# A mixture-of-experts block on one core: the last pair of experts and the last norm written out by themselves

## The reference

```python
h = rms_norm(x, norm1_g);  proj = h @ w_in            # q, k, v, u
sb = rms_norm(stick_breaking_attention(q, k, v));  pool = multiscale_pool(u)
x = x + concat([sb, pool]) @ w_out
h2 = rms_norm(x, norm2_g)
# top 4 of 32 experts per token, softmax over the 4 logits
gu = h2 @ w_gate_up[e] + b_gate_up[e]                 # 1024 -> 2048
gate = minimum(gu[:, :1024], 7);  up = clip(gu[:, 1024:], -7, 7)
y_e = ((up + 1) * gate * sigmoid(1.702 * gate)) @ w_down[e] + b_down[e]
x = x + sum over the token's experts of gate_weight * y_e
return rms_norm(x, final_norm_g)
```

## Time and profile before

| | |
|---|---|
| median of 3 runs | 1057.35 us |
| the profiled execution, its own time | 1059.32 us |
| its span, first to last instruction | 1057.5 us |
| TensorE busy | 993.2 us (94%) |
| VectorE, ScalarE, GpSimd busy | 214.3, 129.3, 8.6 us |
| DMA | 418.43 MB, mean 396 GB/s |
| granted TensorE clock, mean | 0.995 |

### The profile page before, as it was taken

How to read it: one execution, slowest core, us unless ns; L and a number is a source line. 1 busy time by engine, 2 the same in 40 slices (tenths; PEclk the granted TensorE clock), 3 DMA queues, 4 the chain that set the end, 5 groups by cost and what they waited for, 6 DMA issues and landing times.

```text
span 1057.5 us, 11316 instructions
## 1 busy us (share of the span) xinstructions
PE 993.2 (94%) x4595; PEld 421.6 (40%) x4595; DVE 214.3 (20%) x479; ACT 129.3 (12%) x200; POOL 8.6 (1%) x27
## 2 busy tenths in 40 slices
PE   8999999999999999999999989899999989898996
PEld 6684534343433333333333333333334333333333
DVE  2134421112111111111212111111112121111104
ACT  2452200101010001010101000010001010010002
POOL 0001000000000000000000000000000000000000
PEclk9999999999999999999999999999999999999999
DMA  9955379999999999999999999999999999999992
GB/s 326 409 231 195 143 317 420 414 404 428 428 427 426 429 429 429 428 428 430 428 429 428 428 429 428 428 428 429 429 429 428 426 431 429 428 428 428 430 429 115
DMA packets 37826, 418.43 MB, mean 396 GB/s; under 512 B 4600, under 2 KB 5136, under 8 KB 10160
## 3 DMA queue, kind: packets, MB, share of 16 engines
q1 hardware_dynamic: 36320, 417.35, 93.8%
q10 hardware_dynamic: 1488, 0.82, 0.3%
HBM read 417.10 MB, written 1.05 MB: 395 GB/s over the span
## 4 chain that ended last, share of the span: by engine, by line
PE 59%; DMA 32%; DVE 4%; issue 2%; ACT 2%; ACTq 0%; DVEq 0%; SPq 0%
PE bank L942 58%; DMA ring<-in_w_gate_up_dram 32%; DVE area L831 1%; DVE area L828 1%; PE bank L1281 1%; DVE area L781 1%; DMA area<-in_norm_g_dram 1%; DVE area L835 1%; ACT area L526 0%; DVE sel L598 0%; PE bank L965 0%; DVE xn L920 0%; ACT area L447 0%; ACT area L445 0%; ACT area L443 0%
## 5 line engine op out<-in xcount | busy, mean ns | idle before, releaser
L942 PE MATMUL bank<-ring,area 128*64 128x512 f32 (+1 forms) x3088 | 701.2, 597 | 36.8 <-DMA ring<-in_w_gate_up_dram 30.4
L942 PEld LDWEIGHTS bank<-ring,area 128*64 128x64 f32 (+1 forms) x3088 | 220.9, 138 | 484.8 <-issue 410.5
L825 DVE TENSOR_SCALAR area<-bank 128x512 f32<-128x512 f32 x32 | 22.1, 692 | 472.9 <-PE bank L942 472.9
L524 ACT ACTIVATE area<-area 128x512 f32<-128x512 f32 x32 | 20.2, 630 | 503.9 <-DVE area L825 503.9
L942 PE MATMUL bank<-masks,xn 128*128 128x128 f32 x544 | 73.0, 288 | 1.0 <-issue 0.2
L942 PEld LDWEIGHTS bank<-masks,xn 128*128 128x128 f32 x544 | 66.7, 196 | 17.9 <-issue 14.1
L840 DVE COPY wide<-bank 64x512 f32<-64x512 f32 x32 | 22.2, 694 | 205.6 <-PE bank L942 205.6
L529 ACT ACTIVATE wide<-bank 64x512 f32<-64x512 f32 x32 | 18.9, 590 | 254.7 <-PE bank L942 254.7
L942 PE MATMUL bank<-area,ring 128*128 128x256 f32 x192 | 42.0, 380 | 0.3 <-DVE area L616 0.3
L942 PEld LDWEIGHTS bank<-area,ring 128*128 128x128 f32 x192 | 36.3, 190 | 5.4 <-DVE area L616 0.6
L942 PE MATMUL bank<-bias,sel 64*128 64x512 f32 x128 | 37.2, 641 | 0.0
(11 more groups left out here) (137 smaller groups left out, 289.4 us busy)
## 6 DMA issues: line engine op xcount, KB each, us to landing
ring<-in_w_gate_up_dram SPq DMA_DIRECT2D x112, 2048.0 KB, 31.7
ring<-in_w_down_dram SPq DMA_DIRECT2D x56, 2048.0 KB, 35.3
ring<-in_w_gate_up_dram SPq DMA_DIRECT2D x28, 1024.0 KB, 12.5
ring<-in_w_down_dram SPq DMA_DIRECT2D x14, 1024.0 KB, 11.9
ring<-in_w_in_dram SPq DMA_DIRECT2D x8, 512.0 KB, 10.1
ring<-in_w_in_dram SPq DMA_DIRECT2D x4, 1024.0 KB, 18.5
ring<-in_w_out_dram SPq DMA_DIRECT2D x4, 1024.0 KB, 16.9
area<-in_w_gate_up_dram SPq DMA_DIRECT2D x4, 1024.0 KB, 8.1
```

The source lines that it names most:

```text
L524: a.activation(sig, gatec, ACT.Sigmoid, scale=ALPHA).then_inc(sig_ok, 1)
L825: v.tensor_scalar(gatec, gbank[:], LIMIT, None, ALU.min).then_inc(gc, 1)
L942: return t.matmul(o, l, r, start=start, stop=stop, skip_group_check=True)
```

## The change

- The loops end one step earlier. Experts 28 and 29 are written out as they were; experts 30 and 31 have a part of their own (`last_pair`), without a gather behind 31.
- SyncE loads expert 31 in twelve transfers of 1 MB (`load_last`); TensorE waits for each chunk by itself.
- The rows of 30 and 31 are no longer added together. Each expert has a scatter matrix whose 64 slots stand in both halves of the partitions (`pick_twice`, `info_one`, `scatter_one`), and `ylast` puts one half of its columns on partitions 0 to 63, the other on 64 to 127. `combine_one` does four matmuls of 64 rows by 512 columns, alternately on the two halves of the array's rows. Expert 30's come after 31's up steps, 31's at the end.
- The residual is added by four matmuls of the identity with `xres` (`add_tokens`) after the second up step of 31.
- The gain's row goes half after the fourth up step, half after `combine_one(0)`, and ScalarE copies the halves into `fgrow` (`last_gains`), ahead of the sigmoid of expert 31 in its order. The warm-up of the root's table now stands before the copy of expert 31's rows.
- Banks 0 to 3 become one tile `acc`. ScalarE squares 1024 elements at a time right out of it, with no addition of two sums; the last rows are made by VectorE (`fin`) and, for a quarter, by a product of VectorE (`fmul`) and a scaled copy of ScalarE (`fin_a`). Three stores: 512 KB and 256 KB from SyncE, 256 KB from ScalarE.
- In the path not taken, semaphores are renamed.

```diff
+            c = HALF * (r ^ half)
+            return wide[half * SLOTS:(half + 1) * SLOTS, c:c + HALF]
         hidT_all = wide[:].rearrange("p (a b) -> p a b", a=KF)
         wpool = sb("wpool", [P, NG, GC])
         wrouter = sb("wrouter", [P, KD, NE])
...
+
             for r in range(BODY):
                 first_expert(r)
-            with sp.Fori(1, NBODY) as i:
+            with sp.Fori(1, NBODY - 1) as i:
...
-                sp.dma_start(out[0, tt * P:(tt + 1) * P, c:c + HALF],
-                             xn[:, tt, c:c + HALF]).then_inc(out_done, 16)
-            sp.wait_ge(out_done, 64)
+            for r in range(BODY - 1):
+                load_expert(NE - BODY + r, r * PER_EXPERT)
+            load_last(NE - 1, (BODY - 1) * PER_EXPERT)
+            sp.wait_ge(fin, 1)
+            sp.dma_start(out[0, 0:P, :], xn[:, 0, :]).then_inc(out_done, 16)
+            sp.wait_ge(fin, 2)
```

ScalarE and VectorE:

```diff
+            def last_gains():
+
+                for c in (1, 0):
+                    act.wait_ge(gain_ok, 2 - c)
+                    a.activation(fgrow[:, c * HALF:(c + 1) * HALF], (BU, BM)[c][:], ACT.Copy).then_inc(
+                        gain_c, 1)
...
+                fast_hidden(NE - 2)
+                act.wait_ge(chunks_used, (NE - 1) * PER_EXPERT)
+                a.activation(ylast(0, 0), BY[0:SLOTS, :], ACT.Copy).then_inc(y30, 1)
+                last_gains()
+                fast_hidden(NE - 1)
+                a.activation(stat[:, 15:16], epsc[:], ACT.Sqrt).then_inc(warm, 1)
+                act.wait_ge(chunks_used, NE * PER_EXPERT)
+                a.activation(ylast(1, 0), BY[0:SLOTS, :], ACT.Copy).then_inc(y31, 1)
+
+            for tt in range(TT):
+                act.wait_ge(sum_ok, tt + 1)
+                if tt == 1:
+
+                    act.wait_ge(fmul, 1)
+                a.activation(xn[:, tt, :], acc[:, tt, :], ACT.Square,
+                             accum_out=stat[:, 8 + tt:9 + tt]).then_inc(fsq, 1)
+                act.wait_ge(fsq, tt + 1)
                 a.activation(stat[:, 10 + tt:11 + tt], stat[:, 8 + tt:9 + tt], ACT.Sqrt,
                              scale=1.0 / D, bias=epsc[:]).then_inc(frt, 1)
...
+            act.wait_ge(finv, 2)
+            a.activation(xn[:, 1, 0:HALF], xres[:, 1, 0:HALF], ACT.Copy,
+                         scale=stat[:, 11:12]).then_inc(fin_a, 1)
+            act.wait_ge(fin_a, 1)
+            act.dma_start(out[0, P:2 * P, 0:HALF], xn[:, 1, 0:HALF]).then_inc(out_done, 16)
...
+            def pick_twice(e, p):
+
+
+                for tt in range(TT):
+                    for r in range(2):
+                        d = v.tensor_scalar(pick[p][:, tt, r * SLOTS:(r + 1) * SLOTS],
+                                            iota[:, 1:SLOTS + 1], rank[:, tt, e:e + 1], None,
+                                            ALU.is_equal)
+                d.then_inc(pick_ok, 1)
+
+            def scatter_one(r, p):
+
+
+                n = NE // 2 + 1 + r
+                dve.wait_ge(info_ok, n)
+                v.tensor_copy(info[:], BM[:, 0:3]).then_inc(info_c, 1)
+                dve.wait_ge(info_c, n)
+                v.tensor_scalar(scat[p], iota[:], info[:, 2:3], info[:, r:r + 1], ALU.is_equal,
+                                ALU.mult).then_inc(scat_ok, 1)
+
...
+                fast_pair(NE // 2 - 2, 0)
+
+                pick_twice(NE - 2, 0)
+                pick_twice(NE - 1, 1)
+                clamped(NE - 1)
+                choose_bias(NE - 1)
+                scatter_one(0, 1)
+                dve.wait_ge(comb_ok, NE // 2 - 1)
+                dve.wait_ge(scat_ok, NE // 2 + 1)
+                scatter_one(1, 0)
+                dve.wait_ge(chunks_used, (NE - 1) * PER_EXPERT)
+                v.tensor_copy(ylast(0, 1), BY[SLOTS:P, :]).then_inc(y30, 1)
+                clamped(NE)
+                dve.wait_ge(chunks_used, NE * PER_EXPERT)
+                v.tensor_copy(ylast(1, 1), BY[SLOTS:P, :]).then_inc(y31, 1)
...
+            dve.wait_ge(gain_c, 2)
+            dve.wait_ge(sum_ok, 2)
+            v.tensor_tensor(xres[:, 1, 0:HALF], bank[2], fgrow[:, 0:HALF], ALU.mult).then_inc(fmul, 1)
             final_inverse(0)
-            rows_final(0, 0)
-            sum_squares(1)
-            rows_final(0, 1)
+
+            v.scalar_tensor_tensor(out=xn[:, 0, :], in0=acc[:, 0, :], scalar=stat[:, 10:11], in1=fgrow,
+                                   op0=ALU.mult, op1=ALU.mult).then_inc(fin, 1)
             final_inverse(1)
-            rows_final(1, 0)
-            rows_final(1, 1)
+            v.scalar_tensor_tensor(out=xn[:, 1, HALF:D], in0=bank[3], scalar=stat[:, 11:12],
+                                   in1=fgrow[:, HALF:D], op0=ALU.mult, op1=ALU.mult).then_inc(fin, 1)
```

TensorE:

```diff
+            def final_gain(c):
+
+                for r in (2 * c, 2 * c + 1):
+                    m = mm((BU, BM)[c][:, (r % 2) * S:(r % 2 + 1) * S],
                            ident[NE:NE + 4, NE + r:NE + r + 1].to_broadcast([4, P]), fg,
                            start=(r % 2 == 0), stop=(r % 2 == 1))
                 m.then_inc(gain_ok, 1)
...
+            def info_one(r, p):
+
+                n = NE // 2 + 1 + r
+                pe.wait_ge(pick_ok, n)
+                pe.wait_ge(info_c, n - 1)
+                for tt in range(TT):
+                    m = mm(BM[:, 0:3], pick[p][:, tt, :], gtab[:, tt, NE // 2 - 1, :],
+                           start=(tt == 0), stop=(tt == 1))
+                m.then_inc(info_ok, 1)
+
+            def combine_one(r, p, done):
+
+
+                pe.wait_ge(scat_ok, NE // 2 + 1 + r)
+                pe.wait_ge((y30, y31)[r], 2)
+                for tt in range(TT):
+                    for hf in range(2):
+                        m = mm(bank[2 * tt + hf], scat[p][hf * SLOTS:(hf + 1) * SLOTS,
+                                                          tt * P:(tt + 1) * P],
+                               ylast(r, hf), stop=(r == 1))
+                    if r == 1:
+                        m.then_inc(done, 1)
+                if r == 0:
+                    m.then_inc(done, 1)
+
+            def add_tokens():
+
+                for tt in range(TT):
+                    for hf in range(2):
+                        mm(bank[2 * tt + hf], ident[:], xres[:, tt, hf * HALF:(hf + 1) * HALF])
+
+            def last_pair():
+
+                i, q = NBODY - 1, NE // 2 - 1
+                e = NE - 2
+                add_bias_of(e)
+                pe.wait_ge(xb_ok, q + 1)
+                m0 = 2 * PER_EXPERT
+                for k in range(KD):
+                    up_step(i, m0 + k, False, k, 1, slice(0, SLOTS)).then_inc(chunks_used, 1)
+                combine(q - 1, 0)
+                turn_hidden(e)
+                info_one(0, 0)
+                down(i, e, m0, False)
+
+                e = NE - 1
+                add_bias_of(e)
+                m0 = 3 * PER_EXPERT
+                info_one(1, 1)
+                for k in range(KD):
+                    up_step(i, m0 + k, False, k, 1, slice(SLOTS, P), True).then_inc(chunks_used, 1)
+                    if k == 1:
+                        add_tokens()
+                    if k == 3:
+
+                        pe.wait_ge(info_c, NE // 2 + 2)
+                        pe.wait_ge(fg_in, 16)
+                        final_gain(1)
+                combine_one(0, 1, comb30)
+                pe.wait_ge(uc_ok, NE)
+                final_gain(0)
+                turn_hidden(e)
+                down(i, e, m0, False, True)
+                pe.wait_ge(comb30, 1)
+                combine_one(1, 0, sum_ok)
```

More of the change, by code:

```diff
@@ L129, in build, with ylast @@
         g2rows = part(7744, 2 * P)[0:4, :]
+        fgrow = part(2048, D)
         wide = sb("wide", [P, D])
         ypair = wide[:]
+        def ylast(r, half):
+            c = HALF * (r ^ half)
+            return wide[half * SLOTS:(half + 1) * SLOTS, c:c + HALF]
         hidT_all = wide[:].rearrange("p (a b) -> p a b", a=KF)
@@ L174, in build @@
         flag = sb("flag", [1, 1], I32)
-        bank = [ctx.enter_context(nc.psum_tensor(f"bank{i}", [P, HALF], F32)) for i in range(8)]
+        acc = ctx.enter_context(nc.psum_tensor("acc", [P, TT, D], F32))
+        bank = [acc[:, b // 2, (b % 2) * HALF:(b % 2 + 1) * HALF] for b in range(4)]
+        bank += [ctx.enter_context(nc.psum_tensor(f"bank{i}", [P, HALF], F32)) for i in range(4, 8)]
         G1, SBG, PSC = vecT[:, 0:8], vecT[:, 8:12], vecT[:, 12:16]
@@ L889, in _ @@
                 for tt in range(TT):
[L890 to L894, removed]
+                    v.tensor_tensor(acc[:, tt, :], xres[:, tt, :], xn[:, tt, :],
+                                    ALU.add).then_inc(sum_ok, 1)
             with dve.Else():
@@ L897, in _ @@
                 scatter_matrix(0, 0)
-                with dve.Fori(0, NE // BODY) as i:
+                with dve.Fori(0, NBODY - 1) as i:
                     for p in range(2):
                         fast_pair(i * 2 + p, p)
[L901 to L912, removed]
+                fast_pair(NE // 2 - 2, 0)
```

(41 more changed lines are left out.)

128 lines of the change are left out of this document (48 added, 80 removed).

## The result

Over 20 runs each the changed kernel takes 1059.32 us and the kernel before 1057.59 us (medians). The ratio is 1.002 (95% interval 1.0012 to 1.0027), so it is slower by 1.3 to 2.9 us, at the edge of what I called no change. 1058.0 was forecast, with 1056 to 1059.3 as my own range: the measured 1059.32 lies at its upper end.

What follows compares the result with a forecast made beforehand. Weight transfers set the pace until close to the end, then TensorE, VectorE and ScalarE; path to down steps +3.3, tail -3.4, clock making it +0.5; added to 1057.35 and rounded up, 1058.0 us (own range 1056 to 1059.3).

Steps and rivals of the forecast that it cites:

- put among 31's up steps: TensorE, expert 31: info matmuls 0.5, residual matmuls 3.6 and half the gain's row 1.1 add 5.2 us.
- slack of TensorE in 31: Expert 31's up steps: TensorE has 2.6 us of waiting to spare; whatever is added beyond that is paid.
- clamp later, from A: VectorE's first clamp of 31, counted from expert 30's last two up steps: 2.6 us later.
- clamp to down steps: From 31's first clamp to its down steps: 0.7 us longer, the sigmoid waiting behind the gain's copy.
- clock in the down steps: TensorE's clock may fall after little work before 31's down steps: 0 to 1.7 us, taken as 0.6.
- copy of BY to first store: Tail, from the copy of expert 31's rows at 1048.2 to the first store's issue at 1053.25: 5.05 us.
- first store to end: Tail, from first store's issue to span's end: 4.2 us, set by the stores' rate of 385 GB/s.
- the tail, copy of BY to end: From the copy of expert 31's rows to the end: 9.2 us instead of 12.65, a gain of 3.4.
- start A: Start of expert 30's last two up steps, which wait for a transfer: no change up to there, 0 us.
- the row halves one after another: Rival: `combine_one`'s matmuls on the two row halves don't run side by side; 1060.6 us, slower; chance 0.15.
- Fresh code stalling TensorE: Rival: newly loaded code stalls expert 31 or the last combine, a microsecond each; 1060 us, slower; chance 0.08.
- TensorE comes early enough: Rival: TensorE has some 4.5 us more slack, so 31's last chunk sets the end; 1053 us, faster; chance 0.10.

Runs made afterwards that it cites:

- e2: Changed kernel with the residual's four matmuls after the up steps of expert 28 instead of within 31: 1056.9 us, ratio to before 0.9993.
- e1: Changed kernel with expert 31's sigmoid ahead of the copy of the gain's second half on ScalarE: 1056.2 us, ratio to before 0.9997.
- e4: Changed kernel with expert 31 loaded in six 2 MB transfers, TensorE waiting for the pair: 1060.0 us, ratio to before 1.0029.
- e10: Changed kernel with all stores issued from SyncE, none from ScalarE: 1060.4 us, ratio to before 1.002.
- e3: Changed kernel with eight unused matmuls in TensorE's pause before the transposes of 31: 1058.6 us, ratio to before 1.0017.
- e5: Changed kernel with both 31's sigmoid ahead of the gain's second copy and the residual's matmuls after 28's up steps: 1053.8 us, ratio to before 0.996.
- e8: Changed kernel with sigmoid first, residual after 28, first 128 tokens' product halved, gain's row moved to experts 28 and 30: 1052.2 us, ratio to before 0.9954.

## Why the prediction was right

Step by step, in the profile:

| step | forecast | measured |
|---|---|---|
| put among 31's up steps | 5.2 | 0.54 + 3.63 + 1.05 = 5.22 |
| slack of TensorE in 31 | 2.6 | 5.22 - 2.97 = 2.25 |
| clamp later, from A | +2.6 | 36.05 - 33.08 = +2.97 |
| clamp to down steps | +0.7 | 6.37 - 5.74 = +0.63 |
| clock in the down steps | +0.6 | +2.95, in this execution; some +1.2 on the mean |
| copy of BY to first store | 5.05 | 1054.95 - 1049.91 = 5.04 |
| first store to end | 4.2 | 4.45 |
| the tail, copy of BY to end | -3.4 | 9.49 - 12.65 = -3.2 |
| start A | 0 | -1.5, as executions vary |

The sum measured is 2.97 + 0.63 + 2.95 - 3.2 - 1.5 = +1.9, and the spans are 1059.4 and 1057.5. The mechanism was the one forecast: TensorE out of slack in 31 (e2), the sigmoid held by the gain (e1), single loads without worth (e4), a shorter tail that ends at the rate of the stores (e10).

The term that was mis-sized is the clock. I bounded it by one stretch of 3.4 us, as in the rows of before, that is by 1.7, and took 0.6. In this profile it was low for 6.8 and cost 2.95, beyond the bound; the four profiles with this pause (changed, e2, e4, e10) all show the long fall. Over all executions it is less, 1.2 us on the mean by e3 and e4, since not every one has it. One of the changed kernel's has a mean clock of 0.998 in a span of 1054.5 us, which leaves 4.2 us at the low level in all, too little for the long fall. With 1.2 in place of 2.95, and without the start A, the sum is 2.97 + 0.63 + 1.2 - 3.2 = +1.6, and the medians moved by 1.7. I forecast 0.5 in all, rounded up to 0.65. So the mechanism held and the time came out on the right side by little: the clock and the slack fell short by some 1 us together, and the tail gained 0.2 less.

A smaller miss is the slack, 2.25 in place of 2.6: interrupting the up steps twice costs a fresh start each time, so the steps alone took 14.3 us and not 13.9.

Of the rivals, the row halves one after another falls by the 1.99 us for eight instructions. Fresh code stalling TensorE falls too: in the rows after, TensorE has no idle time from 1013.92 to the end of the gain's row, its later waits are ended by VectorE and ScalarE, and the last combine starts after 0.89 us, as in the earlier trace rows. That TensorE comes early enough falls by the missing waits in 31, though e5 shows what an early TensorE and a free sigmoid are worth together: D 3.7 us below before, even with a low clock.

## What to carry to other kernels

Before work is moved into a stage that seems to wait, add up that stage's own wait on the engine (here 2.6 us by the forecast, 2.25 in truth, against 5.2 put in); the same work three experts earlier cost nothing that the profiles show (e5), until the waits there were used up too (e8). When a copy is added to an engine that serves a chain (clamp, sigmoid, product), look at which instruction it stands ahead of, not at its own 0.6 us. And a profile shows one execution: before a fall of the clock is priced from it, look how often the other executions have it.

## What was not expected of the hardware

The granted clock fell to 1.2 GHz after 3.6 us in which TensorE was never idle for more than 2.0 us at a time, but worked only 1.6 us, on matmuls of 4 rows and on transposes, and stayed low for 6.8 us, 6.1 of them busy, nearly all with the down matmuls. The same instructions in other executions don't always bring the fall. A square of 1024 elements straight out of two neighbouring banks (PSUM, where TensorE's sums stand) took 1.02 us on ScalarE, no longer than 1.056 out of `xres` in SBUF, and VectorE's product of 1024 elements 1.28, against 1.41 for two of 512.
